# A two-layer decoder step: attention's values and probabilities split in two f32r halves, and other orders in the recurrent stage

## The reference, cut to what matters

```
def attend_block(i):                      # 4 blocks of 128 queries, all heads
    s = qn @ k_nope + qr @ k_rope
    p = softmax(where(mask, s * SCALE, -inf))
    return einsum('bhqk,bkhd->bqhd', p, v)

def recurrent_mixer(xn, ...):
    z = xn @ w_in                         # xr | gate
    xc = causal_dwconv(xr)                # width 4
    r, gi = sigmoid(block_diag(xc, w_a)), sigmoid(block_diag(xc, w_i))
    a = exp(-8 * r * softplus(-lam)); bx = sqrt(1 - a*a) * gi * xc
    h_t = a_t * h_{t-1} + bx_t
    return (h * gelu(gate)) @ w_out
```

## Time and profile before

| | us |
|---|---|
| median of 3 runs (2001.51 to 2004.55) | 2003.98 |
| the profiled execution | 2000.46 |
| its span | 1998.6 |
| TensorE busy | 1949.0 (98%) |
| VectorE busy | 1040.4 (52%) |
| ScalarE busy | 754.8 (38%) |
| GpSimd busy | 689.0 (34%) |
| DMA, mean | 66 GB/s |

### The profile page before, as it was taken

One profiled execution on the slowest core, in us unless ns is written; L12 is line 12 of the kernel. 1 busy time (PEld: TensorE's weight loads), 2 busy tenths in 40 slices (PEclk: granted clock), 3 DMA queues, 4 the chain that ended last, 5 costly groups with the idle time before them and its releaser, 6 DMA issues.

```text
span 1998.6 us, 36449 instructions
## 1 busy us (share of the span) xinstructions
PE 1949.0 (98%) x13333; PEld 1870.1 (94%) x13333; DVE 1040.4 (52%) x1877; ACT 754.8 (38%) x1525; POOL 689.0 (34%) x682
## 2 busy tenths in 40 slices
PE   7999999999999999999999999999899999999998
PEld 7877659999999999999999999999899999999997
DVE  3676655565556555475335325437845732532542
ACT  4455555554555555322111112246653211211220
POOL 3230002432222233343333333464455333333331
PEclk9998999999999999999999999999999999999999
DMA  5321001111111110222222222232222222222222
GB/s 145 64 64 35 25 5 45 37 37 43 37 38 35 42 39 26 67 82 80 78 85 84 79 80 84 84 95 65 73 72 75 84 82 76 84 85 81 77 85 78
DMA packets 251864, 131.48 MB, mean 66 GB/s; under 512 B 43010, under 2 KB 249539, under 8 KB 251667
## 3 DMA queue, kind: packets, MB, share of 16 engines
q1 hardware_dynamic: 251666, 129.68, 23.3%
q10 hardware_dynamic: 76, 0.18, 0.0%
HBM read 126.21 MB, written 3.61 MB: 65 GB/s over the span
## 4 chain that ended last, share of the span: by engine, by line
PE 92%; DVE 4%; ACT 1%; issue 1%; DMA 1%; POOL 0%; SPq 0%; DVEq 0%; POOLq 0%; ACTq 0%
PE ps L200 20%; PE ps L203 20%; PE ps L201 20%; PE ps L1203 7%; PE ps L1201 7%; PE ps L1202 7%; PE ps L1231 3%; PE ps L981 2%; PE ps L1006 2%; PE ps L1168 1%; PE ps L229 1%; PE ps L997 1%; DVE arena L2081 1%; DMA raw<-in_attn_w_down 1%; DVE arena L772 0%
## 5 line engine op out<-in xcount | busy, mean ns | idle before, releaser
L200 PE MATMUL ps<-split,whi 128*128 128x288 f32 x3024 | 861.1, 298 | 8.8 <-POOL wlo L2272 5.3
L201 PE MATMUL ps<-split,whi 128*128 128x288 f32 x3024 | 851.8, 296 | 0.0
L194 POOL TENSOR_TENSOR wlo<-raw,whi 128x1024 fp32r<-128x1024 f32 x187 | 454.0, 2429 | 636.7 <-ACT whi L171 636.5
L203 PE MATMUL ps<-split,wlo 128*128 128x288 f32 x3024 | 655.3, 297 | 0.0
L200 PEld LDWEIGHTS ps<-split,whi 128*128 128x128 f32 x3024 | 570.4, 189 | 11.9 <-issue 10.9
L201 PEld LDWEIGHTS ps<-split,whi 128*128 128x128 f32 x3024 | 571.5, 189 | 0.6
L203 PEld LDWEIGHTS ps<-split,wlo 128*128 128x128 f32 x3024 | 487.6, 188 | 0.0
L171 ACT CAST whi<-raw 128x1024 fp32r<-128x1024 f32 x187 | 194.9, 1043 | 417.6 <-DMA raw<-in_ffn_w_up 246.8
L1201 PE MATMUL ps<-split,split 128*128 128x384 f32 x768 | 268.2, 349 | 0.0
L1203 PE MATMUL ps<-split,split 128*128 128x384 f32 x768 | 257.9, 336 | 0.0
L1202 PE MATMUL ps<-split,split 128*128 128x384 f32 x768 | 257.2, 335 | 0.0
(11 more groups left out here) (270 smaller groups left out, 2133.3 us busy)
## 6 DMA issues: line engine op xcount, KB each, us to landing
raw<-in_ffn_w_up SPq DMA_DIRECT2D x96, 512.0 KB, 3.8
raw<-in_ffn_w_down SPq DMA_DIRECT2D x48, 512.0 KB, 3.9
arena<-in_cache_ckv SPq DMA_DIRECT2D x128, 128.0 KB, 2.0
raw<-in_rec_w_in SPq DMA_DIRECT2D x16, 512.0 KB, 3.9
raw<-in_attn_w_o SPq DMA_DIRECT2D x8, 512.0 KB, 4.1
raw<-in_rec_w_out SPq DMA_DIRECT2D x8, 512.0 KB, 4.0
raw<-in_attn_w_down SPq DMA_DIRECT2D x7, 512.0 KB, 7.8
raw<-in_attn_w_uq SPq DMA_DIRECT2D x48, 64.0 KB, 2.2
```

What stands on the lines that cost most here:

```text
L194: pool.tensor_tensor(wlo[:, t % RING, :], raw[:, t % RING, :], f32(whi[:, t % RING, :]), ALU.subtract).then_inc(w_lo, 1)
L200: pe.matmul(o, wh, a, start=first, stop=False)
L201: pe.matmul(o, wh, b, start=False, stop=False)
L203: mm = pe.matmul(o, wl, a, start=False, stop=last)
```

## The change

- **Values** are kept in f32r, high and low side by side (128 columns a head): ScalarE writes the high part of all eight blocks, VectorE the low part.
- **Probabilities** are turned four units behind the scores instead of three, and ahead of the scores of the unit. ScalarE writes the turned block's high part (prob_high), ahead of the unit's exp; VectorE its low part (prob_low), ahead of the unit's reduction. GpSimd, not VectorE, scales the probabilities (prompt_pool).
- **attend**: four f32r matmuls with 128 columns of weights (high and low of v) on the high part of p, and four with 64 on the low part. Rows 64 to 127 of the bank hold low v x high p; ScalarE copies them out (half_kept), VectorE adds them to rows 0 to 63 (outputs), now once a head. 
- The low parts of p lie in the ring of raw weights, so w_o's first four tiles are loaded only after the last value product, beside the second sequence's pages.
- **tile_product** does all eight chunks for the first 288 columns and then for the others, except where it waits for its input chunk by chunk, for the half tiles, and for parts. The first weight tile is released in quarters.
- **Recurrent stage**: at n = 1 the gates come behind the gate branch's tile; at n = 7 ScalarE casts ahead of the gates' activations of step 6.
- The rest: buffers moved, some semaphores merged, waits to match.

```diff
-            pe.wait_ge(w_lo, t + 1 + 4 * it)
+            if t:
+                pe.wait_ge(w_lo, t + 1 + 4 * it)
             if a >= 2:
                 pe.wait_ge(acc_free[a % 2], a // 2 + 2 * it)
             wh = whi[:, t % RING, :].rearrange("p (k n) -> p k n", n=P)
             wl = wlo[:, t % RING, :].rearrange("p (k n) -> p k n", n=P)
-            for k in part or range(kn):
-                if ready:
-                    ready(k)
-                mm = product(pe, acc(a % 2), wh[:, at + k, :], wl[:, at + k, :],
-                             halves(xh[:, k, :]), halves(xl[:, k, :]), k == 0, k == kn - 1)
+            both = ready or kn < 8 or part
+            for h in (slice(0, 2),) if both else (slice(0, 1), slice(1, 2)):
+                for k in part or range(kn):
+                    if ready:
+                        ready(k)
+                    mm = product(pe, acc(a % 2)[h], wh[:, at + k, :], wl[:, at + k, :],
+                                 halves(xh[:, k, :])[h], halves(xl[:, k, :])[h], k == 0, k == kn - 1)
...
+                pe.wait_ge(w_lh, k // 2 + 1) if k < 6 else pe.wait_ge(w_lo, 1)
...
+        vals = [area(at + k * 2 * D, NH, 2 * DV, dt=F32R) for at in (A_V, A_P) for k in range(2)]
...
+        def value_high(act, i):
+            act.wait_ge(v_ps, i + 1)
+            act.copy(value_half(i, 0), ps[:, V_BANK[i], :].rearrange("p (h e) -> p h e", e=DV)).then_inc(v_act, 1)
+
+        def value_low(dve, i):
+            dve.wait_ge(v_act, i + 1)
+            dve.tensor_tensor(value_half(i, 1), ps[:, V_BANK[i], :].rearrange("p (h e) -> p h e", e=DV),
+                              f32(value_half(i, 0)), ALU.subtract).then_inc(v_dve, 1)
...
+            for i in range(4):
+                value_low(dve, i)
...
+        pT_hi = area(A_P + 4096, 20, P, dt=F32R)
+        pT_lo = nc.alloc_sbuf_tensor_at("pT_lo", [P, 20, P], F32R, offset=raw_at)
...
         def attend(pe, h):
-            if h >= 2 and h % 2 == 0:
-                pe.wait_ge(p_oev, h // 2)
-            pe.wait_ge(p_tev, 4 * h + 4)
-            r = slice(DV * (h % 2), DV * (h % 2) + DV)
+            if h >= 1:
+                pe.wait_ge(p_oev, 2 * h)
+            pe.wait_ge(p_tlo, 4 * h + 4)
             for kb in range(4):
-                mm = pe.matmul(ps[r, 6, kb * P:TP], vals[:, kb, h * DV:(h + 1) * DV], pT[:, h % 2, kb, kb * P:TP],
-                               start=(kb == 0), stop=(kb == 3))
+                mm = pe.matmul(ps[:, 6, kb * P:TP], vals[kb][:, h, :], queries(pT_hi, h, kb), start=(kb == 0),
+                               stop=(kb == 3))
+                if kb == 0:
+                    for c in range(4):
+                        pe.matmul(ps[0:DV, 6, c * P:TP], vals[c][:, h, 0:DV], queries(pT_lo, h, c), start=False,
+                                  stop=False)
             mm.then_inc(p_o, 1)
...
-        LAG = 3
+        LAG = 4
+        ATTEND = [4 * h + 7 for h in range(NH - 2)] + [4 * NH - 3]
...
+                if u >= LAG:
+                    if u - LAG == UNITS - 1:
+                        pe.wait_ge(k_ln, 8)
+                        turn(pe, 0, 0, 0)
+                    probs_turn(pe, u - LAG)
                 if u < UNITS:
                     h, qb = divmod(u, 4)
                     scores(pe, u)
...
+                if u - LAG in ATTEND:
+                    attend(pe, ATTEND.index(u - LAG))
             attend(pe, NH - 1)
 
         def prompt_act(act):
             for u in range(UNITS + LAG):
+                if u >= LAG:
+                    prob_high(act, u - LAG)
...
+                if u - LAG - 1 in ATTEND:
+                    half_kept(act, ATTEND.index(u - LAG - 1))
+            hi_act(act, 0, 0, 0)
+            half_kept(act, NH - 1)
+
+        def prob_high(act, v):
+            h, qb = divmod(v, 4)
+            act.wait_ge(p_t, v + 1)
+            if qb == 0 and h >= 2:
+                act.wait_ge(p_o, h - 1)
+            act.copy(turned(pT_hi, v), ps[:, 2 + v % 2, 0:(qb + 1) * P].rearrange("p (k q) -> p k q", q=P))\
+               .then_inc(p_tev, 1)
+
+        def prob_low(dve, v):
+            h, qb = divmod(v, 4)
+            dve.wait_ge(p_tev, v + 1)
+            dve.tensor_tensor(turned(pT_lo, v), ps[:, 2 + v % 2, 0:(qb + 1) * P].rearrange("p (k q) -> p k q", q=P),
+                              f32(turned(pT_hi, v)), ALU.subtract).then_inc(p_tlo, 1)
+
+        def prompt_pool(pool):
+            for v in range(UNITS):
+                m = (v % 4 + 1) * P
+                pool.wait_ge(p_inv, v + 1)
+                pool.tensor_scalar(pr[v % 4][:, 0:m], pr[v % 4][:, 0:m], cols[:, 8 + v % 4:9 + v % 4], None,
+                                   ALU.mult).then_inc(p_ok, 1)
+
+        def prompt_dve(dve):
+            for u in range(UNITS + LAG):
                 if u >= LAG:
-                    v = u - LAG
-                    h, qb = divmod(v, 4)
-                    act.wait_ge(p_t, v + 1)
-                    if qb == 0 and h >= 2:
-                        act.wait_ge(p_o, h - 1)
-                    act.copy(pT[:, h % 2, 0:qb + 1, qb * P:(qb + 1) * P],
-                             ps[:, 2 + v % 2, 0:(qb + 1) * P].rearrange("p (k q) -> p k q", q=P)).then_inc(p_tev, 1)
-
-        def prompt_dve(dve):
-            for u in range(UNITS + 1):
+                    prob_low(dve, u - LAG)
                 if u < UNITS:
...
+                if 1 <= u <= UNITS:
                     v = u - 1
-                    m = (v % 4 + 1) * P
                     dve.wait_ge(p_exp, v + 1)
+                    if v >= 4:
+                        dve.wait_ge(p_ok, v - 3)
                     dve.reciprocal(cols[:, 8 + v % 4:9 + v % 4], cols[:, 4 + v % 4:5 + v % 4]).then_inc(p_inv, 1)
-                    dve.wait_ge(p_inv, v + 1)
-                    dve.tensor_scalar(pr[v % 4][:, 0:m], pr[v % 4][:, 0:m], cols[:, 8 + v % 4:9 + v % 4], None,
-                                      ALU.mult).then_inc(p_ok, 1)
...
+                if u - LAG - 2 in ATTEND:
+                    outputs(dve, ATTEND.index(u - LAG - 2))
...
+        def outputs(dve, h):
+            dve.wait_ge(p_oev, 2 * h + 1)
+            if h == 0:
                 dve.wait_ge(s_onat, 64)
-            dve.tensor_copy(oT[:, j, 0:TP], ps[:, 6, :]).then_inc(p_oev, 1)
+            dve.tensor_tensor(oT[DV * (h % 2):DV * (h % 2) + DV, h // 2, 0:TP], ps[0:DV, 6, :], o_half,
+                              ALU.add).then_inc(p_oev, 1)
+
+        def half_kept(act, h):
+
+            act.wait_ge(p_o, h + 1)
+            if h:
+                act.wait_ge(p_oev, 2 * h)
+            act.copy(o_half, ps[DV:2 * DV, 6, :]).then_inc(p_oev, 1)
...
+                    if b and i % 4 == 3:
+                        if i == 3:
+                            sp.wait_ge(p_o, NH)
+                        load_tile(sp, WO0 + i // 4, wo(i // 4))
...
-                rec_gates(pe, n - 1)
+                if n > 1:
+                    rec_gates(pe, n - 1)
                 t = gb_t(n - 1)
                 tile_product(pe, t, t + AOFF, xn_hi, xn_lo).then_inc(w_used, 1)
+                if n == 1:
+                    rec_gates(pe, n - 1)
...
+            if n == DC - 1:
+                act.wait_ge(r_a, 2 * n)
...
+        def rec_cast(act, n):
+            act.wait_ge(r_conv, n + 1)
+            src, dst = prompt_new(xcv[:, n % 2, :], 0), xch[:, n % 2, :]
+            act.copy(dst[:, 0:TP], src[0])
+            act.copy(dst[:, TP:T].rearrange("p (b t) -> p b t", t=TS), src[1]).then_inc(r_hi, 1)
...
+                if n == DC - 1:
+                    rec_cast(act, n)
                 if 1 <= n <= DC:
                     rec_gates_act(act, n - 1)
-                if n < DC:
-                    act.wait_ge(r_conv, n + 1)
-                    src, dst = prompt_new(xcv[:, n % 2, :], 0), xch[:, n % 2, :]
-                    act.copy(dst[:, 0:TP], src[0])
-                    act.copy(dst[:, TP:T].rearrange("p (b t) -> p b t", t=TS), src[1]).then_inc(r_hi, 1)
+                if n < DC - 1:
+                    rec_cast(act, n)
...
-            for d in range(4):
-                load_tile(sp, WO0 + d, wo(d))
             down_store(sp)
-            sample_sp(sp)
+            sample_sp(sp, wo)
...
+                pool.tensor_tensor(wlo[:, 0, c:c + 256], raw[:, 0, c:c + 256], f32(whi[:, 0, c:c + 256]), ALU.subtract)\
+                    .then_inc(w_lh if c < 768 else w_lo, 1)
```

More of the change, by code:

```diff
@@ L467, in down_pe, with first_ready, ready @@
                     down_sum(pe, t - 1)
+        def first_ready(pe):
+            def ready(k):
+                pe.wait_ge(w_lh, k // 2 + 1) if k < 6 else pe.wait_ge(w_lo, 1)
+                pe.wait_ge(n_lo, k + 1)
+            return ready
         def key_rotate(pe):
@@ L882, in values_dve @@
             ins.then_inc(qs_ok, 1)
-            value_kept(dve, dve.tensor_copy, 2, v_dve)
-            value_kept(dve, dve.tensor_copy, 3, v_dve)
-            for k in range(4):
```

(25 more changed lines are left out.)

88 lines of the change are left out of this document (40 added, 48 removed).

## The result

The changed kernel takes 2019.43 us (median of 4 runs, 2017.01 to 2021.22) where the kernel before, beside it, takes 2003.08: ratio 1.0081, 95% interval 1.0064 to 1.0098. It is slower by 16 us; 2015 was forecast. Its profiled execution took 2017.01 us with a span of 2015.2, 16.6 more than before's 1998.6.

A forecast was written before the change was run, and what follows sets the result against it. TensorE's matmul time bounds the kernel before; a ScalarE-VectorE loop would bound attention after. Attention +20.8, values +1.4, first tile -1.1, recurrent stage -9.8, halves 0 make +11.3; 2000.46 + 11.3 + 3.5 = 2015 us, range 1998 to 2036.

The forecast's parts named there:

- The loop: Prompt attention: high, low, reduce, exp run strictly one after another on ScalarE and VectorE, 1.889 us a unit; attention +20.8 us.
- Attention's end: End of prompt attention: the last four turns and two value products take about 6.5 us.
- The values: Ahead of attention: VectorE subtracts all eight value blocks, so the absorbed queries' products start later, +1.4 us (0 to 3).
- the first tile: Kernel start: TensorE waits for all low-weight quarters, then ends the tile at 27.3 instead of 28.4, -1.1 us (-2 to 0).
- GpSimd's scaling: Prompt attention: GpSimd scales probabilities three units ahead of need, hidden even at over twice VectorE's 0.49 us.
- The price of 0.4 for the key norm: Prompt attention: VectorE's key norm, reading two SBUF operands beside GpSimd, takes 0.4 us longer each (0 to 0.8).
- The recurrent stage: Recurrent stage: two new orders fill TensorE's holes of 3.98 and 9.42 us, 11.0 less 1.2: -9.8 us (-5 to -11).
- The column halves: tile_product in about 157 tiles: halves in turn change nothing, 0 us, with ends of -6.5 and +6.
- The first: Rival, attention: the two engines' loop doesn't close and TensorE still sets the pace; total 1978 us, 13 in 100.
- The second: Rival, attention: the clock falls with TensorE partly idle, +2 us a pair or more; total 2033 us, 16 in 100.
- The third: Rival, tile_product: the column halves cost 6 us; total 2021 us, 8 in 100.
- The fourth: Rival: the halves give 6.5 us and the recurrent stage all its 11; total 2007 us, no difference, 11 in 100.

The follow-up runs named there:

- e12: e5 with ScalarE's last half_kept behind the first sequence's query_act and VectorE's sums of heads 13 and 14 ahead of their unit's prob_low: 1982.10 us, ratio 0.992.
- e5: Changed kernel with VectorE's reduction of unit u moved ahead of prob_low of u-4, ScalarE's order kept: 1983.79 us, ratio 0.9906 to the kernel before.
- e6: Changed kernel with the probabilities scaled on VectorE behind its reciprocal, GpSimd idle in attention: 2022.15 us, ratio 1.0092 to the kernel before.
- e3: Kernel before with only the two recurrent orders, first-step gates behind the gate branch's tile and last-step cast ahead of its tanh: 1992.27 us, ratio 0.995.
- e11: e5 with column halves in the FFN stages alone and ScalarE's last half_kept behind the first sequence's query_act: 1984.62 us, ratio 0.9921 to the kernel before.

## Why the forecast came out right, point by point

**The loop: the turn right, what stands in it mis-sized.** The turn was put at 1.889 us. In after the four steps without anything else beside them are 1.49, 1.54, 2.02 and 2.50 us, 7.55 together, 1.888 each. Key_square adds 0.57 and key_root 1.26, as forecast. Without the end's 6.5 the terms come to 146.0, and they reach to the end of the last unit's exp; measured that is 149.4 (165.54 to 314.98, the first row below), 3.4 more. A pair is 18.9 by these terms (the 18.1 of the prediction leaves the key norm out) and took 19.44. half_kept costs 0.74 a head (2.28 for 1.54) instead of 0.47, since its record doesn't overlap its neighbours' as I had assumed (it starts at 250.70, after exp's read, and high at 251.30, after its end). VectorE's excess from the key copy is 0.47 a pair (2.49 for 2.02) instead of 0.22. The key norm goes the other way, 0.55 instead of 0.78. The value products take 1.3 us at full clock (311.8 to 313.1), TensorE is idle for 18% of the steady part where I had said a quarter.

**Attention's end: mis-sized.** I gave 6.5 to the last four turns and two products. From the end of the last exp to the end of the last product it is 10.7 (the 14.6 of the table are counted from the last scores, which start 3.4 ahead of that exp). With the 3.4 of the loop this makes the 7.7 by which attention's two stages lie over the forecast. These rows of after's timeline show it:

```profile
314.29 0.69 ACT L1086 ACTIVATE work<-ps,cols 128x512 f32<-128x512 f32 x1 [1.36 <-DVE cols L1128]
...
317.45 0.79 PE L1040 MATMUL ps<-split,split 128*128 128x512 f32 x1 [3.24 <-DVE arena L1155]
...
320.76 0.48 ACT L1102 CAST split<-ps 128x384 fp32r<-128x384 f32 x1 [4.53 <-PE ps L1020]
...
324.20 0.49 PE L1040 MATMUL ps<-split,split 128*128 128x512 f32 x1 [1.99 <-DVE arena L1155]
...
325.12 0.57 PE L1040 MATMUL ps<-split,split 128*128 128x384 f32 x3
...
327.81 0.41 PE L1266 MATMUL ps<-split,split 128*128 128x384 f32 x1 [1.88 <-DVE qr_s L1353]
```

At the end no scores stand between the products, so each product (L1040) waits for the product before it to be copied out, kept and added (L1163, L1155), a chain that I had counted nowhere; in before a bank held two heads and the last product waited for none of this. Behind the first wait the matmuls run at the lower clock. And the first page product waits 1.88 us for casts that stand behind half_kept on ScalarE: 2.0 that I had put at nothing. e12 took back 1.7 and 3.9 of e5's by order alone.

**The values: mis-sized; the first tile: lost in the scatter.** The first scores come at 164.8 to 168.6 in the eight profiles with the new values, mean 166.9, and at 163.0 to 165.7 in the six without, mean 164.4: +2.5 for a forecast of +0.3. The two groups scatter by 3.8 and 2.8 us, but most of that lies ahead of the first sums of the down stage. From there on it takes 129.2 to 131.8 with the new values and 126.5 to 128.6 without, means 130.6 and 127.7: +2.9 for the +1.4 (0 to 3) that I gave the values. What in them costs it stays open. The first sums come at 35.4 to 37.7 over all profiles, so the first tile's 1.1 can't be told (0.6 between after and before, 35.54 for 36.14).

**GpSimd's scaling: hidden in the loop, right.** e6 shows it; with the loop open, in e5, it is in the chain. The price of 0.4 for the key norm was too high (0.06): I had taken it from a row beside GpSimd's weight splits, which read two operands and last 2.4 us, while the scaling reads one and starts behind the key norm. Which of the two makes the difference no run separates.

**The recurrent stage: -9.8 forecast, -6.0 in e3, -4.1 in after.** The start of the last gates was right (1444.1 to 1445.1; in e3 1439.0, with everything ahead of it 5.1 earlier, so 1444.1). Wrong was what followed: gates_act(7) starts 1.0 later than put, since casts and a weight split stand ahead of it on ScalarE; its joins run beside GpSimd; and each new hole costs the clock besides its own length, where I had let TensorE go on at full pace.

**The column halves: the step that failed.** I took 0 between -6.5 and +6, and with -12.3 in the two FFNs they lie outside my bounds; both FFN stages moved by over 3 us, which I had set as a sign of being wrong. I had the row for what would go, 134.5 in the loops, but took 133.3 from w_o's one-bank form as what would come, and thought it a matter of loops. It is 132.5: 144 tiles of 48 matmuls by 1.9 ns are 13.1. My 6.5 were 1.2 ns in some 113 tiles, while nearly all of the 144 tiles of both FFNs ran at 134.4, those in straight code too. Had I followed the pace along the whole trace, 130.0 here and 134.4 there, I would have seen that this order had more than one pace.

**The rivals.** The first (TensorE sets the pace) fell with the pair of 19.44. The second named a real thing, the clock: 0.96 in 180 to 270, and 0.87 in 270 to 318, under the 0.95 that I had set as a sign against me. But in 214 to 222, where it was 0.60, the pair took 19.44 as well: TensorE had that time to spare in the loop. It cost something only at the end, where products stand in the chain. The third fell. The fourth was right on the halves' sign, and they gave twice its 6.5.

**The sum.** By the table's rows the part up to the FFN, forecast at +21.1, is +33.0, and the rest, forecast at -9.8, is -16.4: one 11.9 too low, the other 6.6 too high, which leaves the 5.3 by which the spans differ from the forecast. "Slower" stood on that too: with the halves at their true worth and all else as I had it, I would have forecast 2003, no difference. The mechanism of the loop was right; that the total lay only 4 us off was luck, two misses of opposite sign.

## What to carry to other kernels

When two in-order engines feed each other, write the ring of waits down unit by unit, with the index of each: one operation moved past another may close or open it, and no engine's busy time shows it. Check the end of a pipelined stage by itself, since what was covered by the next unit's work stands bare there. And before a change in the order of matmuls, read their start-to-start time over the whole trace, not at one place.

## What the runs showed of the hardware

- The same f32r matmuls of 288 columns, with the same loads and at full clock, run at 130.0, 131.8 or 134.4 ns each over whole stages, and at 132.5 in a part of w_o's product, when two PSUM banks alternate within a chunk; when one bank is filled at a time, at 132.5 with the halves in turn and at 133.3 in w_o's first tiles. What sets the pace of the first form isn't known from these runs: it is neither loop nor straight code. The Trainium skill, in "TensorE: Matmul & The Clock Gate", "Back-to-back issue gap", gives an isolated gap of columns over 2.4 GHz and 2.5 ns; an estimate by it is 122.5 ns here, 7.5 to 12 under all of them.
- VectorE's operations with two SBUF operands are held up by GpSimd's splits, and the other way round, by which of the two starts first: the same subtraction took 2.87 us in e11, where GpSimd was 0.08 us ahead, and 0.76 in after, where GpSimd, 0.08 behind, took 2.93 for the 2.34 of e11. Its lateness alone cost TensorE 2.8 in e11. Of three operations in the recurrent stage one of 0.21 us took 1.45 in e3. The Trainium skill says so in "SBUF — State Buffer", "SBUF: two separate sides": whichever starts first holds the shared port pair for its whole instruction. The recurrent and FFN rows agree. Beside the scaling, which has one such operand, less was lost than a whole instruction on either side: 0.12 us by the second instruction of the key norm, 0.49 by GpSimd.
- GpSimd's scaling takes 0.92 us for 256 columns (1.41 beside the key norm, 1165 ns as the mean of both in 180 to 270 us) and 1402 ns as a mean of the blocks of 384 and 512, where VectorE takes 353 and 454.
